# Compressed attention by head pairs, masks as products, and respread pieces of stick-breaking and delta rule

## The chip, the cores and the metric

The kernel runs on one core of one Trainium2 chip. What counts is the device time of one execution in microseconds (us). The core has five engines that run their own instruction streams and meet through semaphores: TensorE (PE in the profile), VectorE (DVE), ScalarE (ACT), GpSimd (POOL) and SyncE (SP, here only DMA issue). A product on PE has two halves, the load of the stationary operand (PEld) and the pass of the moving one (PE).

## What is computed

Two transformer blocks follow each other, each of two layers, on 512 tokens of width 1024. The first block mixes latent attention, sparse attention (DSA, 4 heads) and retention, then a feed-forward part. The second block mixes a gated delta rule (6 heads), a native sparse attention (NSA, 6 heads on 2 key groups) and stick-breaking attention (4 heads), then a convolutional feed-forward part. The parts that the change touches, from the reference:

```python
# NSA: compressed keys and values, one per 16 tokens (31 of them), then two causal attentions
kc = compress(rope(kv(k_cmp), positions), pe_k, ck_w1, ck_w2)
vc = compress(kv(v_cmp), pe_v, cv_w1, cv_w2)
s_c = jnp.einsum('bqgrd,bigd->bgrqi', qb, kc).astype(f32) * scale
p_c = masked_softmax(s_c, cmp_end[None, :] <= tq[:, None])
o_c = jnp.einsum('bgrqi,bigd->bqgrd', p_c.astype(vc.dtype), vc)
# stick-breaking, per head
log_stick = lax.cumsum(log_1m, axis=3, reverse=True) - log_1m
a = jnp.where(strict, jnp.exp(jax.nn.log_sigmoid(z) + log_stick), 0.0)
return jnp.einsum('bhqk,bkhd->bqhd', a.astype(v.dtype), v)
# gated delta rule, per chunk of 64 tokens: S is the state
S_t = exp(g_t) (I - beta_t k_t k_t^T) S_{t-1} + beta_t k_t v_t^T
```

## The kernel before

The program is a row of stages. Each stage is a block in which every engine has its own instruction list, and a barrier closes it, so a stage ends with its slowest engine. The order inside a stage is written out by hand: the loops below are it. Token tiles are 128 rows (four tiles, `TT`), a PSUM bank holds 512 columns. In each layer of the second block the stages around the change follow in this order.

**Compressed attention** (`turned_and_compressed`). PE turns queries and keys, makes the compressed keys and values and then, for each of 6 heads and 4 token tiles, the scores against 31 compressed keys (L3256, contraction over 64 rows, 31 moving columns). DVE adds the mask (L3368), takes maxima, subtracts (L3373), ACT exponentiates (L3320), DVE masks again (L3378) and signals `masked`. Then the tail: for each head PE turns four tiles of weights (L3269), ACT copies them out of PSUM (L3325), PE multiplies them with the values (L3278), DVE scales the result into its place (L3390). Beside it ACT and DVE split the queries into a high and a low part (L3295, L3348) for the next stage. PE is kept moving before the tail by 26 transposes without use (L164).

**NSA attention** (`softmax_attention`, name `nsa`). 12 heads (6 heads, two key sets), four tiles each, software pipelined over units of one head and tile: scores as two reduced-precision products (L2362), for tiles 2 and 3 the causal mask as a third product (L2365), for tiles 0 and 1 the mask as a DVE addition in PSUM (L2400), maximum (L2401, DVE), exponential (L2431, ACT), transposes (L2374, PE), copy (L2440, ACT), output products (L2384, PE). The first block's DSA stage is the same function with four heads, where tiles 1 and 2 have product masks and tiles 0 and 3 additions.

**Stick-breaking** (`stick_breaking`). 16 units of head and key tile. PE: scores (L3422), running sums (L3433, L3441), and, five units after the last unit of a head, its ten output products in one piece (L3453). DVE: mask (L3495), softplus (L3504), total (L3512), and beside it the NSA head norm in large pieces (L3514, L3517, four L3521, L3526). The running sums wait for the softplus.

**Delta rule** (`gated_delta`). First `transpose_tiles` turns 12 sets of 128 columns (L486) while DVE scales keys and queries (L3874, L3875), POOL makes two faded copies of the keys (L3878, L3880), and the turned sets are copied out of PSUM by ACT (even sets, L508) and DVE (odd sets, L525). Then `delta_inverse`, where POOL starts with a memset (L2983) and one addition per head (L2988), and `delta_scan`, which alone reads the faded keys.

## Time and profile before

| | us |
|---|---|
| three runs, median (lowest to highest) | 3344.66 (3342.47 to 3351.53) |
| the profiled execution, its own time | 3343.76 |
| its span, first to last instruction | 3341.8 |
| PE busy in the span | 3172.3 (95%) |
| DVE busy | 1839.2 (55%) |
| ACT busy | 1303.3 (39%) |
| POOL busy | 390.2 (12%) |
| mean granted TensorE clock | 0.978 of full |

A busy time is the time in which an engine had an instruction in work. PE is busy nearly always, but its time is not fixed: at half of the clock the same product takes twice as long and is still busy. So the profile is read stage by stage, with the granted clock beside the busy time, and with what each engine waited for. Stages are found by the names of their tensors: `cmp` for the compressed attention, `nsa`, `stick`, `b_work` and `b_kbe` for the delta rule.

### The profile page before, as it was taken

The numbers are of one execution on the slowest core, as the hardware profiler recorded it, in microseconds if no ns is written. First come the engines' busy times: TensorE is split into PE (matmuls) and PEld (weight loads), VectorE is DVE, ScalarE is ACT, GpSimd is POOL, SyncE is SP. The second block draws the span as 40 slices with busy tenths as digits, with TensorE's granted clock in tenths as the row PEclk, the third lists the DMA queues.
The fourth block names the chain that finished last, engine by engine and source line by source line (L and its number), as shares of the span: only waits on it lengthen the run. The fifth ranks groups of instructions, "written<-read, shape, count | busy, mean of one in ns | idle before, by whom it ended". The sixth has DMA issues, their size and how long they took to land. (4 is left out here: it accounts for less than half of the span.)

```text
span 3341.8 us, 48972 instructions
## 1 busy us (share of the span) xinstructions
PE 3172.3 (95%) x19264; PEld 2667.0 (80%) x19264; DVE 1839.2 (55%) x3260; ACT 1303.3 (39%) x2690; POOL 390.2 (12%) x354
## 2 busy tenths in 40 slices
PE   8999999999999999979999999999899989999996
PEld 6877788877877888868877888888788868888885
DVE  4875443436864434247466457474475565474644
ACT  4454433334354424234363333233443643332324
POOL 1021000000030000003013302010003034010100
PEclk9999999999999999989899999999999899999998
DMA  4111222222202222132100123222232000232231
GB/s 167 54 51 39 89 96 94 88 78 82 71 1 76 101 88 101 38 123 96 51 1 2 40 76 98 96 101 86 73 104 76 1 1 15 82 103 93 92 103 39
DMA packets 37341, 239.54 MB, mean 72 GB/s; under 512 B 4464, under 2 KB 5232, under 8 KB 15088
## 3 DMA queue, kind: packets, MB, share of 16 engines
q1 hardware_dynamic: 36528, 234.21, 20.6%
q8 instruction: 158, 2.59, 0.3%
q10 hardware_dynamic: 576, 2.10, 0.2%
q14 instruction: 79, 0.65, 0.1%
HBM read 234.19 MB, written 2.10 MB: 71 GB/s over the span
## 5 line engine op out<-in xcount | busy, mean ns | idle before, releaser
L265 PE MATMUL ps<-b_hl,bff_whl 128*128 128x512 f32 x704 | 274.2, 389 | 3.1 <-DVE b_hl L665 3.1
L267 PE MATMUL ps<-b_hl,bff_whl 128*128 128x512 f32 x704 | 274.0, 389 | 0.0
L266 PE MATMUL ps<-b_hl,bff_whl 128*128 128x512 f32 x704 | 273.9, 389 | 0.0
L248 DVE SCALAR_TENSOR_TENSOR bff_whl<-ring,b_cols,bff_whl 128x512 fp32r<-128x512 f32 (+1 forms) x224 | 153.2, 745 | 197.3 <-ACT bff_whl L235 197.0
L245 DVE TENSOR_TENSOR aff_whl<-ring,aff_whl 128x512 fp32r<-128x512 f32 x160 | 99.9, 687 | 224.8 <-ACT aff_whl L233 224.8
L235 ACT ACTIVATE bff_whl<-ring,b_cols 128x512 fp32r<-128x512 f32 (+1 forms) x224 | 136.6, 681 | 176.4 <-PE ps L267 176.4
L266 PE MATMUL ps<-aff_whl,a_u 128*128 128x512 f32 x512 | 204.3, 399 | 0.0
L265 PE MATMUL ps<-a_hl,aff_whl 128*128 128x512 f32 x512 | 200.8, 392 | 3.1 <-DVE a_hl L665 3.1
L265 PE MATMUL ps<-aff_whl,a_u 128*128 128x512 f32 x512 | 201.8, 394 | 0.0
L267 PE MATMUL ps<-aff_whl,a_u 128*128 128x512 f32 x512 | 200.7, 392 | 0.0
L266 PE MATMUL ps<-a_hl,aff_whl 128*128 128x512 f32 x512 | 200.5, 392 | 0.0
L267 PE MATMUL ps<-a_hl,aff_whl 128*128 128x512 f32 x512 | 200.5, 392 | 0.0
L265 PE MATMUL ps<-ain_whl,a_hl 128*128 128x512 f32 (+3 forms) x512 | 189.3, 370 | 8.4 <-issue 5.2
L233 ACT CAST aff_whl<-ring 128x512 fp32r<-128x512 f32 x160 | 87.5, 620 | 278.6 <-PE ps L267 272.5
L266 PE MATMUL ps<-ain_whl,a_hl 128*128 128x512 f32 (+3 forms) x512 | 186.3, 364 | 0.0
L267 PE MATMUL ps<-ain_whl,a_hl 128*128 128x512 f32 (+3 forms) x512 | 186.0, 363 | 0.0
L245 DVE TENSOR_TENSOR bff_whl<-ring,bff_whl 128x512 fp32r<-128x512 f32 x128 | 84.7, 722 | 144.3 <-ACT bff_whl L233 144.2
L265 PEld LDWEIGHTS ps<-b_hl,bff_whl 128*128 128x128 f32 x704 | 132.2, 188 | 31.0 <-DVE b_hl L665 3.6
L248 DVE SCALAR_TENSOR_TENSOR aff_whl<-ring,a_gains,aff_whl 128x512 fp32r<-128x512 f32 x128 | 87.6, 747 | 125.5 <-ACT aff_whl L235 125.3
L267 PEld LDWEIGHTS ps<-b_hl,bff_whl 128*128 128x128 f32 x704 | 132.2, 188 | 27.4
L266 PEld LDWEIGHTS ps<-b_hl,bff_whl 128*128 128x128 f32 x704 | 132.2, 188 | 27.3
L233 ACT CAST bff_whl<-ring 128x512 fp32r<-128x512 f32 x128 | 70.4, 621 | 210.4 <-PE ps L267 202.9
(521 smaller groups left out, 7804.7 us busy)
## 6 DMA issues: line engine op xcount, KB each, us to landing
ring<-in_a_w_ff SPq DMA_DIRECT2D x64, 1024.0 KB, 4.8
ring<-in_b_w_up SPq DMA_DIRECT2D x32, 1024.0 KB, 5.0
ring<-in_a_w_in SPq DMA_DIRECT2D x16, 1024.0 KB, 5.4
ring<-in_b_w_down SPq DMA_DIRECT2D x16, 1024.0 KB, 4.8
ring<-in_b_w_in_att SPq DMA_DIRECT2D x12, 1024.0 KB, 4.9
ring<-in_b_w_up SPq DMA_DIRECT2D x16, 768.0 KB, 4.2
ring<-in_b_w_in_conv SPq DMA_DIRECT2D x12, 768.0 KB, 4.4
ring<-in_a_w_out SPq DMA_DIRECT2D x8, 1024.0 KB, 4.9
```

The source lines that it names most:

```text
L233: self.c.nc.scalar.copy(self.part(j, 0, k), src[:, k, :]).then_inc(self.hi_made, 1)
L235: self.c.nc.scalar.activation(self.part(j, 0, k), src[:, k, :], ACT.Copy, scale=g[:, row + k:row + k + 1]).then_inc(self.hi_made, 1)
L245: self.c.nc.vector.tensor_tensor(self.part(j, 1, k), src[:, k, :], self.part(j, 0, k).bitcast(F32), ALU.subtract).then_inc(self.lo_made, 1)
L248: self.c.nc.vector.scalar_tensor_tensor(out=self.part(j, 1, k), in0=src[:, k, :], scalar=g[:, row + k:row + k + 1], in1=self.part(j, 0, k) ...
L265: nc.tensor.matmul(bank, sh, mh, start=start, stop=False)
L266: nc.tensor.matmul(bank, sh, ml, start=False, stop=False)
L267: return nc.tensor.matmul(bank, sl, mh, start=False, stop=stop)
```

## The change

It changes only the stages named above. No load, no weight product and no feed-forward part is touched.

1. Compressed attention by pairs of heads. Keys and values of two heads stand on the diagonal of one block (`kc` 128 rows by 2 times 32 columns, `vc` 64 rows by 128 columns), the rest is zero. Scores are 12 products over 128 rows and 64 columns in place of 24 over 64 rows and 31 columns; the tail has three turns instead of six. POOL clears the blocks, DVE fills them with four small copies each. The query lows of heads 2 to 5 move into the NSA stage.
2. All causal and selection masks of the NSA and DSA stages are products; DVE's additions there are gone.
3. Stick-breaking: the output products of a head are issued in three pieces over three units, its copy out of PSUM one unit later, and the norm's large DVE pieces are cut by token tile.
4. Delta rule: DVE copies out only sets 2, 5 and 8 of the twelve, ACT the others; the faded keys are made by POOL in eight pieces inside `delta_inverse`, the second from the product of beta and decay (`beg`).

```diff
@@ turned_and_compressed, PE
-                for h in range(H):
-                    b, gr = HD * (h % 2), h // NSA_R
-                    bank, at = score_at(h)
+                for a in range(A):
+                    bank, at = score_at(a)
                     for t in range(TT):
-                        ins = nc.tensor.matmul(c.ps[:, bank, at + t * N:at + (t + 1) * N],
-                                               qT[b:b + HD, h // 2, t * P:(t + 1) * P],
-                                               kcT[b:b + HD, gr * N:(gr + 1) * N], start=True, stop=True)
+                        ins = nc.tensor.matmul(c.ps[:, bank, at + t * 2 * NW:at + (t + 1) * 2 * NW],
+                                               qT[:, a, t * P:(t + 1) * P],
+                                               kc[:, a].rearrange("p b n -> p (b n)"), start=True, stop=True)
...
@@ DVE, the diagonal blocks and the two query lows that stay
+                for b in range(2):
+                    r, ones = slice(HD * b, HD * (b + 1)), group_of(b).index(1)
+                    ins = spread([(kc[r, 0:ones, b, 0:N], 0), (kc[r, ones:A, b, 0:N], 1)],
+                                 c.ps[r, SMALL, 128:128 + G * N].rearrange("p (g n) -> p g n", g=G))
...
+                query_low(0)
+                query_low(1)
                 for i in range(13, len(turns), 2):
                     keep(i)
...
@@ attentions, the NSA heads
-                              lambda j, a=v + h // NSA_R * HD: proj[:, j, a:a + HD], lambda t: c.causal if t < 2 else None,
+                              lambda j, a=v + h // NSA_R * HD: proj[:, j, a:a + HD], lambda t: None,
...
-                              lambda t: (mask_product[0][:], mask_product[1][:]) if t >= 2 else None)
+                              lambda t: (mask_product[0][:], mask_product[1][:]))
+                beside=lambda dve, done, i: queries.low(dve, done, 2 + i // 4) if i in (0, 4, 8, 12) else None,
+                ready=lambda pe, done, h: pe.wait_ge(done, h - 1) if 2 <= h < NSA_H else None)
@@ stick_breaking, PE
-                    u = i - 5
-                    if 0 <= u < U and units[u][1] == 0:
+                    for late, tiles in ((5, (0, 1)), (6, (2,)), (7, (3,))):
+                        u = i - late
+                        if not (0 <= u < U and units[u][1] == 0):
+                            continue
@@ stick_breaking, DVE
-                    if i == 3:
-                        nc.vector.tensor_tensor(sq[:], xo, xo, ALU.mult).then_inc(squared, 1)
+                    if 2 <= i < 2 + TT:
+                        t = i - 2
+                        nc.vector.tensor_tensor(sq[:, t], xo[:, t], xo[:, t], ALU.mult).then_inc(squared, 1)
...
@@ gated_delta
-            nc.gpsimd.tensor_tensor(as4(g["kel"]), k4, wide(g["el"]), ALU.mult)
-            pool.wait_ge(made, 1)
-            nc.gpsimd.tensor_tensor(as4(g["kbe"]), as4(g["kb"]), wide(g["eg"]), ALU.mult)
-        transpose_tiles(c, "deltaT", jobs, faded, None, scaled, wait_scaled)
+            nc.gpsimd.tensor_tensor(g["beg"], g["beta"], g["eg"], ALU.mult)
+        transpose_tiles(c, "deltaT", jobs, faded, None, scaled, wait_scaled, (2, 5, 8))
```

The order of the instructions shows it at three places. The first is PE from the compressed scores to the start of the NSA stage. `cmpkcT` and `cmpkc` are the compressed keys, `cmps` the weights, `cmppT` the turned weights, `cmpvcmp` and `cmpvc` the values. Before:

```order
L3256 MATMUL ps<-cmpkcT,b_qT 128x31 x24
L3215 MATMUL ps<-const_b,b_proj 128x128 x12
L164 MATMUL ps<-const_b 128x128 x26
L3269 MATMUL ps<-const_b,cmps 31x128 x8
L3278 MATMUL ps<-cmpvcmp,cmppT 128x64 x4
L3269 MATMUL ps<-const_b,cmps 31x128 x4
L3278 MATMUL ps<-cmpvcmp,cmppT 128x64 x4
```

(Three more such pairs follow, and a last product group of eight.) In the changed kernel:

```order
L3262 MATMUL ps<-cmpkc,b_qT 128x64 x12
L3221 MATMUL ps<-const_b,b_proj 128x128 x12
L164 MATMUL ps<-const_b 128x128 x26
L3275 MATMUL ps<-const_b,cmps 64x128 x8
L3285 MATMUL ps<-cmpvc,cmppT 128x128 x4
L3275 MATMUL ps<-const_b,cmps 64x128 x4
L3285 MATMUL ps<-cmpvc,cmppT 128x128 x8
```

The tail is now 12 transposes and 12 products of twice the moving columns, in place of 24 and 24.

The second place is DVE in the first units of the stick-breaking stage, where `sticksq` and `stickssq` belong to the NSA norm. Before:

```order
L3512 TENSOR_TENSOR ps<-ps,stickz 128x256
L3514 TENSOR_TENSOR sticksq<-b_mix 128x1536
L3495 TENSOR_TENSOR stickz<-ps,stickhide 128x128
L3504 SCALAR_TENSOR_TENSOR sticksp<-stickz,sticke 128x512
L3512 TENSOR_TENSOR ps<-ps,stickz 128x384
```

In the changed kernel, the same stretch:

```order
L3545 TENSOR_TENSOR ps<-ps,stickz 128x256
L3548 TENSOR_TENSOR sticksq<-b_mix 128x384
L3528 TENSOR_TENSOR stickz<-ps,stickhide 128x128
L3537 SCALAR_TENSOR_TENSOR sticksp<-stickz,sticke 128x512
L3545 TENSOR_TENSOR ps<-ps,stickz 128x384
L3548 TENSOR_TENSOR sticksq<-b_mix 128x384
L3552 TENSOR_REDUCE stickssq<-sticksq 128x6
```

A quarter of the squares stands where the whole stood, and the other quarters are in the units around.

The third is POOL from the turning stage of the delta rule into `delta_inverse`. Before:

```order
L3878 TENSOR_TENSOR b_kel<-b_qkv,b_g_el 128x1536
L3880 TENSOR_TENSOR b_kbe<-b_work,b_g_eg 128x1536
L151 UNCONDITIONAL_BRANCH
L2981 UNCONDITIONAL_BRANCH
L2983 MEMSET b_work 64x24x64
L2988 TENSOR_TENSOR b_work<-b_work,const_b 128x256 x6
```

In the changed kernel:

```order
L3921 TENSOR_TENSOR b_beg<-b_g_beta,b_g_eg 128x24
L151 UNCONDITIONAL_BRANCH
L2982 UNCONDITIONAL_BRANCH
L2984 MEMSET b_work 64x24x64
L3926 TENSOR_TENSOR b_kel<-b_qkv,b_g_el 128x384 x4
L2991 TENSOR_TENSOR b_work<-b_work,const_b 128x256
L3926 TENSOR_TENSOR b_kbe<-b_qkv,b_beg 128x384
L2991 TENSOR_TENSOR b_work<-b_work,const_b 128x256
```

The two large products have left the turning stage and stand in eight quarters behind its closing barrier (the two branches), the last four between the additions of the heads.

## Rows read from the trace of the kernel before

**Rows 1.** The page: busy time and share; granted TensorE clock in 40 slices.

```profile
PE 3172.3 (95%) x19264; PEld 2667.0 (80%) x19264; DVE 1839.2 (55%) x3260; ACT 1303.3 (39%) x2690; POOL 390.2 (12%) x354
...
PEclk9999999999999999989899999999999899999998
```

**Rows 2.** Busy time by stretch, stick-breaking of both layers: engines, then PEclk, DMA.

```profile
1729.00:1781.00 52.00, 46.90 (x195) 30.21 (x194) 31.17 (x63) 29.07 (x65) 13.93 (x18) 0.87 0.00 1
...
2669.00:2717.00 48.00, 42.34 (x194) 27.34 (x194) 30.92 (x62) 29.08 (x65) 13.93 (x18) 0.96 0.00 1
```

**Rows 3.** The same view in stretches of 2 us, compressed tail, both layers.

```profile
1650.00:1652.00 2.00, 2.00 (x15) 1.69 (x14) 1.11 (x2) 0.57 (x1) 0.00 (x0) 0.86 0.00 0
...
2588.00:2590.00 2.00, 2.00 (x10) 1.43 (x9) 0.91 (x2) 0.00 (x0) 0.00 (x0) 0.50 0.00 0
```

**Rows 4.** Timeline, compressed stage, second layer: start, us, engine, line, [idle before].

```profile
2575.20 3.41 PE L3256 MATMUL ps<-cmpkcT,b_qT 64*128 64x31 f32 x48 [0.61 <-DVE cmpkcT L3359]
...
2584.01 0.93 DVE L3378 TENSOR_TENSOR cmps<-cmps,const_b 128x744 f32<-128x744 f32 x1 [1.84 <-ACT cmps L3320]
...
2587.05 1.96 PE L3278 MATMUL ps<-cmpvcmp,cmppT 31*128 31x64 f32 x8 [1.00 <-ACT cmppT L3325]
...
2588.95 1.06 PE L3269 MATMUL ps<-const_b,cmps 128*31 128x128 f32 x4
...
2602.31 0.42 DVE L3390 TENSOR_TENSOR b_mix<-ps,cmpst 128x256 f32<-128x256 f32 x1 [0.56 <-PE ps L3278]
...
2603.05 0.44 PE L2362 MATMUL ps<-b_khi,b_qhl 128*128 128x128 f32 x1 [0.78 <-PEq L151]
```

**Rows 5.** Timeline, the same tail in the first layer.

```profile
1646.13 0.93 DVE L3378 TENSOR_TENSOR cmps<-cmps,const_b 128x744 f32<-128x744 f32 x1 [3.13 <-ACT cmps L3320]
...
1649.18 1.10 PE L3278 MATMUL ps<-cmpvcmp,cmppT 31*128 31x64 f32 x8 [1.00 <-ACT cmppT L3325]
...
1663.30 0.44 PE L2362 MATMUL ps<-b_khi,b_qhl 128*128 128x128 f32 x1 [0.78 <-PEq L151]
```

**Rows 6.** Timeline, products of the new shapes' kind at full clock.

```profile
2567.74 3.91 PE L3226 MATMUL ps<-b_kv2T,ring 128*128 128x66 f32 x32
...
2728.21 1.16 PE L2846 MATMUL ps<-b_work 64*128 64x128 f32 x8
...
2729.20 1.05 PE L2846 MATMUL ps<-b_dqT,b_work 64*128 64x128 f32 x8
```

**Rows 7.** Timeline, one head of the NSA stage in its steady state.

```profile
2628.11 0.30 DVE L2400 TENSOR_TENSOR ps<-ps,const_b 128x128 f32<-128x128 f32 x1 [1.14 <-PE ps L2362]
...
2629.95 0.22 PE L2365 MATMUL ps<-b_causalr,b_identr 128*128 128x128 f32 x1
...
2630.01 0.28 PE L2374 MATMUL ps<-const_b,nsap 128*128 128x128 f32 x1
...
2631.83 0.41 PE L2374 MATMUL ps<-const_b,nsap 128*128 128x128 f32 x2 [0.35 <-ACT nsapT L2440]
```

**Rows 8.** Stick-breaking: PE's waits (total, times, longest) of both layers; one DVE piece.

```profile
PE ps L3433 <- DVE sticksp L3504: 3.9, 5, 1.2
...
PE ps L3433 <- DVE sticksp L3504: 4.7, 7, 1.2
...
2675.45 1.75 DVE L3514 TENSOR_TENSOR sticksq<-b_mix 128x1536 f32<-128x1536 f32 x1
```

**Rows 9.** Timeline, turning stage of the delta rule, second layer.

```profile
2717.19 2.76 POOL L3878 TENSOR_TENSOR b_kel<-b_qkv,b_g_el 128x1536 f32<-128x1536 f32 x1 [9.19 <-POOLq L151]
2717.21 4.36 DVE L3874 TENSOR_TENSOR b_work<-b_qkv,b_g_beta 128x1536 f32<-128x1536 f32 x1 [0.72 <-PEq L151]
...
2721.49 1.75 DVE L3875 TENSOR_TENSOR b_work<-b_qkv,b_g_eg 128x1536 f32<-128x1536 f32 x1
...
2725.55 1.28 DVE L525 TENSOR_SCALAR b_qeT<-ps 128x512 f32<-128x512 f32 x2
...
2727.15 1.13 PE L2839 MATMUL ps<-const_b,b_g_gcum 128*128 128x128 f32 x8 [0.85 <-PEq L151]
```

210 lines of the change are left out of this document (121 added, 89 removed).

## The prediction

> **What bounds the kernel now.** The page comes first. PE is busy for 3172.3 of 3341.8 us and DVE for 1839.2 [rows 1], so over the whole program a faster DVE, ACT or POOL is worth nothing by itself. The row of granted clocks reads 9 nearly everywhere, with a few 8s [rows 1]. Since a product at half of the clock is busy for twice the time, the next view is the one by stretches, for the stages of the change. There PE's clock is 0.96 in the stick-breaking of layer 2 and 0.87 in that of layer 1, and the second takes 52 us in place of 48 with the same work [rows 2]. In the compressed tail PE is busy without a gap and its clock is 0.50, the lower level (1.2 of 2.4 GHz), in layer 2, and on its way there in layer 1 [rows 3]. So three things can be won: PE work and its time at half clock (compressed tail), waits of PE (stick-breaking, NSA), and a stage that another engine ends (the turning stage of the delta rule, where DVE's last copies end [rows 9]). Every term below occurs in each of two layers. The sums are made against the profiled execution, 3343.76 us; the median of the runs is 0.9 us above it, which is less than I can resolve.
>
> **1. The compressed tail.** The path is: DVE masks the weights (end of L3378), ACT copies turned weights, PE multiplies and turns, DVE scales the last result (L3390), the barrier, first NSA product. In layer 2 the mask ends at 2584.01 + 0.93 = 2584.94 and NSA starts at 2603.05, 18.1 us later [rows 4]. In layer 1 it is 1647.06 to 1663.30, 16.2 us [rows 5]. The first eight value products take 1.96 us in layer 2 and 1.10 in layer 1 [rows 4, 5]: the clock had already fallen in the one, and in the other it fell within 1650 to 1652, where 0.86 as a mean puts the fall 0.56 us before the end, at 1651.4 or 4.4 us after the mask [rows 3].
>
> The new tail starts like the old: eight turns, and the first product 2.1 us after the mask (2587.05 and 1649.18 [rows 4, 5]), because ACT's copy of the turned weights stands before it. Then come four products, four turns and eight products, the products now 64 rows by 128 columns. That form is in the trace: the next group of L2846 starts 0.99 us after one of eight records, which are four products, since a full-precision product has two records (24 scores are 48) [rows 4, 6]. The old group of 64 columns costs 1.10, so the price goes by the product and not by its columns, and at half clock it is 1.96 [rows 4, 5]: I take 1.0 us for four new products and 2.0 at half clock. Four turns are 1.06 us at half clock [rows 4] and 0.53 at full. So PE needs 1.0 + 0.53 + 2.0 = 3.5 us at full clock and 7.1 at half. To that the 2.1 us before it, 0.1 to reach DVE, about 0.7 for a last scaling of 512 columns (an estimate from 0.42 for 256 [rows 4] and 0.64 for a plain copy of 512 [rows 9]) and 0.3 from its end to the next stage, as 2602.73 to 2603.05 now [rows 4]. The tail is 6.8 us at full and 10.3 at half clock. The mask itself comes 0.3 us later, for four small copies more on DVE (about 0.1 each); the scores pay part of that back: 24 products of 64 rows cost 3.41 us (48 records [rows 4]), 12 over 128 rows are 24 records of at most 0.122 (3.91/32 [rows 6]), 2.9 us.
>
> Layer 2, with the clock falling when it did: 18.1 - 10.3 - 0.3 = 7.5 saved (11.0 at full clock). Layer 1, with the fall 4.4 us after the mask, which leaves only the last group at half: end at 7.9, 16.2 - 7.9 - 0.3 = 8.0 (5.6 all at half, 9.1 at full). I take **-15.5**, between -13 and -20. A full clock at the start of NSA would add up to 4. The query lows that stay on DVE hide under ACT's exponentials; if that cover were gone, they would cost 0.64 each [rows 9], 2.6 in all.
>
> On the scores one rule bears. The row shows 3.41/48 = 0.07 us a record for contractions over 64 rows and 0.122 for 128 [rows 4, 6]. The Trainium skill, page "TensorEngine Tiling (Array Packing)", section "Key Properties", says that different tiles of the array can load and multiply in parallel. By it the block diagonal, which fills the whole array with half zeros, gives away an overlap that the old form had. The trace agrees in that a 64-row record is cheaper, but not at more than the halved count gives back. By the rule alone this step would be a wash, by the rows a gain of 0.5 us a layer; no more than 1 us of the sum hangs on it.
>
> **2. Stick-breaking.** PE waits for the softplus five times for 3.9 us in layer 1 and seven times for 4.7 in layer 2, the longest 1.2 [rows 8]. What delays the softplus is that DVE works off pieces of up to 1.75 us for the norm (L3514 [rows 8]) ahead of it; now the pieces are a quarter, 0.44. The rest of the waits lies at the first units after a head, where running sums are due quickly while the ten output products stand in one piece at another place; they are now spread over three units, which gives the chain to softplus more cover. I take two thirds of the waits, 3.0 + 2.6 = 5.6. Then the clock: 0.87 over 52 us is 13.5 us at half, 0.96 over 48 is 3.8 us [rows 2], and each costs half of itself, 8.7 together. Its fall follows stretches in which PE stands, so fewer waits mean fewer falls; I take 4, which is what layer 1 is longer than layer 2 [rows 2]. Together **-9.5**. Bounds: -2, if the wait moves to the ACT link of the chain, since ACT (29 us of 48) is as loaded as DVE (31 [rows 2]); -15, if all 8.6 of waits and 6 of the clock return.
>
> **3. The turning stage of the delta rule.** DVE's product L3874 takes 4.36 us while POOL's L3878 (2.76) starts with it, and L3875, the same size, takes 1.75 afterwards [rows 9]: 2.76 + 1.6. Without POOL's product there both take 1.75, DVE is free 2.6 us earlier, and copies out three sets in place of six (0.64 each [rows 9], 1.9 less). DVE would then be done 4.5 us earlier, at about 2722.4; but ACT now copies nine sets and PE's turns are not faster, so these are late next. With nine at 0.6 or so in a row behind the first turned sets I put the end at about 2724 instead of 2726.83 (2725.55 + 1.28). That is 2.9 a layer, **-5.8**, between -4 and -6.5. The eight quarters on POOL (2.76/4 = 0.69 each) stand behind the memset in the inverse stage, which POOL enters idle (9.19 us of idle time before L3878 [rows 9] shows how little it has to do around here). If they hit DVE's products there, eight per layer and half of them on the path, it would be 4 × 0.7 × 2 = 5.6 us back; I hold this out of the sum and put it into the range.
>
> The lock shows here as 4.36 against 1.75 [rows 9]. The Trainium skill, page "SBUF — State Buffer", section "🔬 SBUF: two separate sides", states that a DVE instruction with two SBUF inputs and a GpSimd instruction that reads SBUF hold a shared pair of ports exclusively, for the whole instruction. The trace agrees. By it moving POOL's products is worth something only where DVE has no such product beside them; by its strict reading the quarters would give back up to 5.6 us.
>
> **4. NSA.** 24 heads (12 in each layer). Tiles 0 and 1 get a mask product each, as tiles 2 and 3 have: 0.06 us by the distance to the next product (2629.95 to 2630.01), at most 0.12 [rows 6, 7]. DVE loses two additions of 0.30 per head, the one at 2628.11 behind its own wait, and PE's wait of 0.35 for ACT's copy once per head [rows 7] is the end of the chain that ran through them. A head then gives 0.35 - 0.24 = 0.11 to 0.35 - 0.12 = 0.23; over the 20 heads without a late query low 2.2 to 4.6, say 2.6. Four heads (two in each layer) do a query low (0.64 [rows 9]) together with the norm work of the stage before, some +0.4 each, +1.6. **-1**, from -5 to +8 (no wait returned, all products at 0.12, and 0.64 lost in each of four heads).
>
> **5. DSA of the first block.** The same with 4 heads in each of 2 layers, 8 × 0.1: **-0.8**, from -3 to +1.
>
> The sum is 15.5 + 9.5 + 5.8 + 1 + 0.8 = 32.6, and 3343.76 - 32.6 = **3311**.
>
> **The rivals.** *Waits only move.* In stick-breaking the softplus waits for ACT, not DVE, and the clock stays low through the whole short tails. Then -12 (tail), -2 (stick), -4 (delta), 0 (NSA, DSA): 18 us, 3326. For it: ACT and DVE are nearly equally busy there [rows 2], and the clock in the tail was 0.50 [rows 3]. Against it: the largest wait has the length of a DVE piece [rows 8].
>
> *The clock holds.* With denser products and fewer stands PE keeps 2.4 GHz in tail, NSA start and stick-breaking: 20 + 4 + 15 + 6.5 + 2 = 47 us, 3297. For it: the clock fell late in layer 1's tail [rows 3]. Against it: the wait before the tail (1.00 us [rows 4, 5]) remains.
>
> *The mask products are no bargain.* NSA and DSA lose 9, and the others stand at their lower ends, 13 + 2 + 4: 10 us, 3334, within 0.3%. For it: PE is the bound, and this gives it work. Against it: 0.06 us in the row [rows 7].
>
> *Slower.* The place is the NSA stage behind the shorter tail, the mechanism the clock: the tail leaves it at 0.50 [rows 3], and if it stays there, each us of a bound PE loses half. To be slower by 10 us it must lose 33 + 10 = 43, so the clock would have to stay low for over 86 us in all. Against it: the slices of the page after both tails read 9 [rows 1], behind the same 0.50.
>
> **How the numbers follow.** Forecast 3311: 0.51 (its own range 3303 to 3320). Waits only move, 3326: 0.25. The clock holds, 3297: 0.17. Mask products no bargain, 3334: 0.05. Slower: 0.02. The range for 8 in 10 goes from 3296 to 3328: it takes in the second and third case and the 5.6 us of the lock. 0.3% (10 us) is about what a measurement of this kernel can tell from no change; faster by more has 0.51 + 0.25 + 0.17 = 0.93, within it 0.05, slower 0.02.
>
> **What the profile after would show.** Step 1: 7 to 10 us from the mask to the first NSA product, where 18.1 and 16.2 stand. Step 2: PE's waits for the softplus at some 1.5 us a layer in place of 3.9 and 4.7, and the clock of the layer 1 stretch near 0.97. If they are shorter but new waits for ACT stand beside them, the first rival is right. Step 3: L3874's successor at 1.75 us and a last copy 3 us earlier; a POOL quarter beside a lengthened DVE product in the inverse stage would show the lock. Step 4: the 0.35 us before L2374 gone, no new wait before it, and mask slots of 0.06. The forecast is wrong above all if the value products of 128 columns are not 0.25 us each, or if the clock in tail and stick-breaking behaves otherwise than it did.

## The result, and the profile after

The changed kernel takes 3300.15 us in the median of three runs (3296.66 to 3302.26), where the kernel before took 3344.66. The ratio is 0.9869, with a 95% interval of 0.9845 to 0.9892. That is faster, as forecast, and inside the range of 3296 to 3328, but the gain is 44.5 us where 33.7 were forecast. The profiled execution has a span of 3298.4 us in place of 3341.8, that is 43.4 less.

The page first: the row of PE's busy time, and the granted clock in 40 slices, to be read against [rows 1].

```profile
PE 3144.2 (95%) x19216; PEld 2651.6 (80%) x19216; DVE 1812.1 (55%) x3220; ACT 1302.5 (39%) x2692; POOL 391.2 (12%) x374
...
PEclk9999999999999999989999999999999999999998
```

PE has 28.1 us less of busy time with only 48 records fewer, so most of that is not work that went away but work that ran at a higher clock; the other 15.3 us are time in which PE stood, that is, had nothing in work. The stages tell where. This is the view by stretches with one stretch per stage, in the order DSA, compressed attention, NSA, stick-breaking, turning stage of the delta rule, each in its second layer. The columns after the comma are the busy times of PE, PEld, DVE, ACT and POOL with their records, then the clock, the DMA share and GB/s. The kernel before:

```profile
988.09:1013.98 25.89, 22.06 (x169) 19.72 (x169) 15.91 (x35) 14.70 (x49) 7.72 (x4) 1.00 0.00 1
2557.07:2603.05 45.98, 41.50 (x374) 37.53 (x375) 24.91 (x44) 18.03 (x31) 3.56 (x2) 0.82 0.14 47
2603.05:2669.59 66.54, 61.88 (x488) 58.02 (x489) 42.24 (x120) 44.12 (x145) 0.00 (x0) 0.97 0.00 1
2669.59:2717.21 47.62, 42.34 (x195) 27.34 (x195) 30.64 (x62) 29.05 (x65) 13.95 (x19) 0.96 0.00 1
2717.21:2727.15 9.94, 6.74 (x57) 6.06 (x57) 9.62 (x8) 3.59 (x6) 7.00 (x3) 1.00 0.00 0
```

The changed kernel:

```profile
983.48:1007.49 24.01, 23.04 (x176) 20.79 (x177) 13.26 (x27) 14.62 (x49) 7.72 (x4) 1.00 0.00 1
2531.82:2569.39 37.57, 32.74 (x318) 30.11 (x319) 21.41 (x46) 16.34 (x28) 5.04 (x5) 0.88 0.17 57
2569.39:2634.26 64.87, 62.69 (x512) 60.67 (x513) 38.71 (x100) 43.67 (x145) 0.00 (x0) 0.97 0.01 1
2634.26:2677.33 43.07, 40.28 (x194) 26.52 (x195) 30.62 (x70) 29.17 (x65) 13.28 (x19) 1.00 0.00 1
2677.33:2683.94 6.61, 6.31 (x57) 6.10 (x57) 5.30 (x5) 4.84 (x9) 0.27 (x2) 1.00 0.00 0
```

With the first layers, read from the same view:

| stage | before, layer 1 / 2 | after, layer 1 / 2 | forecast, both | measured, both |
|---|---|---|---|---|
| compressed attention | 46.14 / 45.98 | 37.56 / 37.57 | -15.5 | -17.0 |
| stick-breaking | 51.57 / 47.62 | 43.06 / 43.07 | -9.5 | -13.1 |
| turning stage of the delta rule | 9.94 / 9.94 | 6.61 / 6.61 | -5.8 | -6.7 |
| NSA | 66.58 / 66.54 | 65.10 / 64.87 | -1 | -3.2 |
| DSA | 27.38 / 25.89 | 24.09 / 24.01 | -0.8 | -5.2 |
| sum | | | -32.6 | -45.0 |
| all other stages | | | 0 | +1.6 |

Every term has the forecast sign and every one is larger than forecast. A stage's length times what its mean clock lacks of 1 is what the lower clock cost there; over these stages that is about 32 us before and 13 after, so some 19 of the 45.0 us are clock. That part is the one that varies between executions of the same stage, and each number here is from one execution. The other stages differ by up to 3 us in either direction, mostly with their clock (the stretch between the two layers took 661.3 us before and 664.3 after). One small stage ahead of the DSA search takes 6.83 us in place of 6.63 at full clock in every kernel with the change, a cost of 0.4 us in all that I had not seen.

The compressed tail, on PE and then DVE, second layer:

```profile
2559.63 1.42 PE L3275 MATMUL ps<-const_b,cmps 128*64 128x128 f32 x8 [2.23 <-DVE cmps L3407]
2561.56 2.07 PE L3285 MATMUL ps<-cmpvc,cmppT 64*128 64x128 f32 x8 [0.51 <-ACT cmppT L3332]
...
2564.56 3.78 PE L3285 MATMUL ps<-cmpvc,cmppT 64*128 64x128 f32 x16
2569.39 0.45 PE L2363 MATMUL ps<-b_khi,b_qhl 128*128 128x128 f32 x1 [1.05 <-PEq L151]
...
2558.51 1.07 DVE L3407 TENSOR_TENSOR cmps<-cmps,const_b 128x248 f32<-128x248 f32 x3 [0.20 <-ACT cmps L3327]
```

The mask ends at 2559.58 and NSA starts at 2569.39: 9.8 us, where [rows 4] gave 18.1. A group of four products of 128 columns takes 2.07 us at half clock, where I had taken 2.0. Ahead of the tail PE stands for 2.23 us, in both layers. In the kernel before it stood there too, for 2.09 us in the second layer, and for only 0.85 in the first, which no row of mine had shown:

```profile
1647.12 1.06 PE L3269 MATMUL ps<-const_b,cmps 128*31 128x128 f32 x8 [0.85 <-DVE cmps L3378]
...
2585.00 1.06 PE L3269 MATMUL ps<-const_b,cmps 128*31 128x128 f32 x8 [2.09 <-DVE cmps L3378]
```

### The profile page after: what moved, and what is told of

The parts are those of the page before. It is cut to its first block and busy times, and to the rows that moved or that the text cites. A ratio compares the mean times of both kernels' runs of the same rounds, so it can differ in the third digit from the quotient of the medians.

```text
span 3298.4 us, 48870 instructions
## 1 busy us (share of the span) xinstructions
PE 3144.2 (95%) x19216; PEld 2651.6 (80%) x19216; DVE 1812.1 (55%) x3220; ACT 1302.5 (39%) x2692; POOL 391.2 (12%) x374
```

## Stick-breaking: which of the two pieces, and what the clock adds

Two kernels undo one part of the change each. The first gives DVE its large pieces back:

```diff
-                    if 2 <= i < 2 + TT:
-                        t = i - 2
-                        nc.vector.tensor_tensor(sq[:, t], xo[:, t], xo[:, t], ALU.mult).then_inc(squared, 1)
+                    if i == 3:
+                        nc.vector.tensor_tensor(sq[:], xo, xo, ALU.mult).then_inc(squared, 1)
...
+                    if i == 12:
+                        nc.vector.tensor_tensor(xo, xo, ssq[:].unsqueeze(3).broadcast_to(shape), ALU.mult)
```

> The changed kernel with one part undone: in stick-breaking DVE does the norm of the stage before in its large pieces again (one of 1536 columns for the squares, one for their sums, four for the gain, one of 1536 for the last factor). The output products of a head stay spread over three units. Reference points for the stage, from barrier to barrier: 51.6 and 47.6 us before (granted clock 0.87 and 0.96), 43.1 and 43.1 after (clock 1.00 in both). Theory D (the large DVE pieces delay the softplus, PE stands, and the clock falls after it): the two waits of about 1.2 us return, the clock falls again in at least one layer, the stage takes 46 to 50 us, and the kernel is 5 to 12 us slower than the changed one. Theory P (the ten output products in one piece are what starves the chain to the softplus): the stage stays at 43 to 44.5 us at clock 1.00, and the kernel within 3 us of the changed one.

It is slower than the changed kernel: 0.9924 of the kernel before (0.9902 to 0.9945), where the changed one has 0.9869, some 13 us by the medians and more than the 5 to 12 expected. The two layers run the same instructions, and this is what the view by stretches has for them, and for three stretches within the second:

```profile
1713.27:1757.83 44.56, 40.28 (x195) 26.52 (x195) 30.57 (x62) 29.11 (x65) 13.95 (x19) 1.00 0.00 1
2630.98:2684.80 53.82, 49.62 (x194) 31.97 (x195) 31.11 (x61) 29.26 (x65) 13.94 (x19) 0.81 0.00 1
2643.00:2646.00 3.00, 1.98 (x8) 1.01 (x7) 2.69 (x5) 1.45 (x3) 0.71 (x2) 1.00 0.00 0
2646.00:2649.00 3.00, 2.38 (x6) 1.52 (x6) 2.25 (x5) 2.87 (x9) 2.06 (x3) 0.54 0.00 0
```

And the piece of PE's timeline ahead of the fall, with the two large DVE pieces behind which the softplus stood:

```profile
2639.86 1.10 PE L3462 MATMUL ps<-sticksp,const_b 128*128 128x512 f32 x2 [1.19 <-DVE sticksp L3537]
2644.93 0.67 PE L3462 MATMUL ps<-sticksp,const_b 128*128 128x256 f32 x2 [1.02 <-DVE sticksp L3537]
2646.86 1.62 PE L3462 MATMUL ps<-sticksp,const_b 128*128 128x384 f32 x2 [0.62 <-DVE sticksp L3537]
...
2636.83 1.75 DVE L3547 TENSOR_TENSOR sticksq<-b_mix 128x1536 f32<-128x1536 f32 x1
2642.25 1.74 DVE L3550 TENSOR_REDUCE stickssq<-sticksq 128x24 f32<-128x1536 f32 x1
```

PE's waits for the softplus are 3.9 us in six places in either layer, in place of 2.4 us in the changed kernel. In layer 1 that costs 44.56 - 43.06 = 1.5 us and nothing else. In layer 2 the same waits were followed by a granted clock of 0.50 (the lower level, 1.2 GHz) from 2646 to about 2667, and the stage took 10.8 us longer than in the changed kernel, 9.3 of them by the clock. So a wait has a small price that is certain and a large one that comes in some executions of a stage and not in others.

The second kernel has the small DVE pieces and the ten output products in one piece again:

```diff
-                    for late, tiles in ((5, (0, 1)), (6, (2,)), (7, (3,))):
+                    for late, tiles in ((5, (0, 1, 2, 3)),):
...
-                    if 0 <= i - 4 < U and units[i - 4][1] == 1 and units[i - 4][0] >= 1:
+                    if 0 <= i - 3 < U and units[i - 3][1] == 1 and units[i - 3][0] >= 1:
```

> The counterpart: the changed kernel with the ten output products of a head in one piece again, five units after its last unit, and their copy out of PSUM one unit earlier; DVE's norm pieces stay cut by token tile. Theory D: the stage stays at 43 to 44.5 us, clock 1.00. Theory P: the stage goes back to 46 to 50 us, the waits of PE for the softplus rise from 2.4 us a layer to 3.5 or more, and the clock falls below 0.97 in at least one layer. If both parts are needed, this one and its counterpart each give about half, 45 to 46 us.

```profile
1712.87:1757.80 44.93, 40.72 (x195) 26.17 (x195) 30.44 (x70) 28.93 (x65) 13.27 (x19) 1.00 0.00 1
2631.52:2676.44 44.92, 40.71 (x194) 26.17 (x195) 30.43 (x70) 28.92 (x65) 13.27 (x19) 1.00 0.00 1
```

The stage takes 1.9 us more in both layers, with PE's waits at 3.6 us in eight places and one more of 0.3, and the clock stays full. The total does not show it (0.9869, interval 0.9847 to 0.989): 3.7 us is less than such a comparison can tell. Both parts are worth something, and neither theory has it alone. At full clock the stage of the kernel before takes 45.9 us: that is measured, in the run with 34 transposes below, whose stick-breaking is that of the kernel before and whose second layer had clock 1.00. So of the 13.1 us, 2 x 2.9 = 5.8 come back at full clock, nearly all of them waits, and 7.3 are clock.

The 7.3 belongs to this pair of executions. In the run with 34 transposes the same stage took 47.60 and 45.94 us, and against these the changed kernel gains 7.4 us, of which 1.7 are clock. What holds over all runs is how often the clock fell: in three of the four layers with the old stage, and in one of the twenty layers of the ten kernels that have the new one (44.71 us at clock 0.96, in the second layer of the next experiment).

## DSA: one addition of 512 columns

Here the forecast was farthest off. The experiment gives tile 3 its addition on DVE back, and only that (a third edit, not shown, lets the search write this tile's mask where the addition reads it):

```diff
-                                        lambda t: None,
+                                        lambda t: search.tile(3) if t == 3 else None,
...
-                                        mask_products=lambda t: (identr[:], search.mask(t) if t else causalr[:]))
+                                        mask_products=lambda t: (identr[:], search.mask(t) if t else causalr[:]) if t < 3 else None)
```

> The changed kernel with the search mask of tile 3 in the DSA stage added by DVE again (512 columns in PSUM) while tile 0 keeps its mask product. The DSA stage took 27.4 and 25.9 us before, 24.1 and 24.0 after, where I had forecast a gain of only 0.4 us a layer. Theory A (the one addition of 512 columns, 0.70 us, once per head in front of the maximum, made PE wait for ACT four to five times): PE's waits for ACT go back to 2.5 us or more and the stage to 25.5 us or more. Theory B (tile 0's addition of 0.30 was as much to blame, since it stands at the head's change): waits of 1.0 to 1.5 us, stage near 25 us.

```profile
276.48:303.64 27.16, 23.93 (x173) 21.48 (x173) 15.60 (x31) 14.66 (x49) 7.72 (x4) 0.94 0.00 1
989.36:1016.08 26.72, 23.51 (x173) 21.05 (x173) 15.51 (x31) 14.73 (x49) 7.72 (x4) 0.95 0.00 1
```

The stages take 27.16 and 26.72 us where the changed kernel has 24.09 and 24.01, and PE waits for ACT's copy four times for 2.4 us, longest 1.1, and once for its exponential for 0.4. The kernel is at 0.9891 of the one before (0.9867 to 0.9916), which by itself can't be told from the changed kernel; the stage can. The cause is to be seen in the trace of the kernel before, DVE and PE:

```profile
1007.30 0.70 DVE L2400 TENSOR_TENSOR ps<-ps,a_score 128x512 f32<-128x512 f32 x1 [0.69 <-PE ps L2362]
...
1009.94 0.63 PE L2374 MATMUL ps<-const_a,dsap 128*128 128x128 f32 x4 [1.11 <-ACT dsapT L2440]
```

The addition stands in front of the maximum, the maximum in front of the exponential, and so on to PE; at the end of the stage nothing is left to run beside that chain, and its whole length is PE's wait. A clock of 0.95 over 26.7 us is a tenth of it at half clock, 1.3 us lost, so at full clock the stage would be near 25.4 (worked out, not measured). Then 1.4 of the 1.9 us between 25.89 and 24.01 are tile 3's, and the rest tile 0's. Theory A held. The clock fell in both layers of this run and in one of the kernel before.

## The turning stage: the lock and the split

Two kernels again, one with POOL's copies back in the stage, one with the old division of the copies out of PSUM:

```diff
         def faded(pool, made):
-            nc.gpsimd.tensor_tensor(g["beg"], g["beta"], g["eg"], ALU.mult)
+            nc.gpsimd.tensor_tensor(as4(g["kel"]), k4, wide(g["el"]), ALU.mult)
+            pool.wait_ge(made, 1)
+            nc.gpsimd.tensor_tensor(as4(g["kbe"]), as4(g["kb"]), wide(g["eg"]), ALU.mult)
```

> The changed kernel with POOL's two faded copies of the keys back in the turning stage of the delta rule, each in one instruction, and no quarter in the inverse stage. The split of the copies out of PSUM stays the new one (DVE sets 2, 5 and 8). Turning stage 9.94 us before, 6.61 after. Theory lock (POOL's product holds DVE's off): DVE's first product takes about 4.4 us again in place of 1.75, and the stage takes 9 us or more, because POOL itself (2.8 + 2.8 us and a wait) also ends late; the kernel is 4 to 6 us slower. Theory split (what mattered was DVE copying out three sets in place of six): the stage takes 7 to 7.5 us. The same run takes the eight quarters out of the inverse stage (77.5 and 74.6 us after, 76.0 and 76.3 before): if they cost anything there, it falls by up to 2.8 us a layer; I expect under 0.5 at the same clock.

```diff
-        transpose_tiles(c, "deltaT", jobs, faded, None, scaled, wait_scaled, (2, 5, 8))
+        transpose_tiles(c, "deltaT", jobs, faded, None, scaled, wait_scaled)
```

> The changed kernel with the old division of the copies out of PSUM in the turning stage of the delta rule (DVE the odd sets, six of twelve), POOL's products staying in the inverse stage. Turning stage 6.61 us after, 9.94 before. By my forecast DVE is free 2.6 us earlier than before without POOL's product, so the old split alone gives about 7.3 us (9.94 - 2.6); the new split would then be worth 0.7 us a layer. Theory lock alone: 7.0 to 7.6. Theory split: 9 us or more.

DVE's first product of the stage in the changed kernel, and then DVE's and POOL's with POOL's copies back:

```profile
2677.33 1.83 DVE L3915 TENSOR_TENSOR b_work<-b_qkv,b_g_beta 128x1536 f32<-128x1536 f32 x1 [0.71 <-PEq L151]
```

```profile
2672.99 4.37 DVE L3915 TENSOR_TENSOR b_work<-b_qkv,b_g_beta 128x1536 f32<-128x1536 f32 x1 [0.72 <-PEq L151]
...
2672.98 2.77 POOL L3921 TENSOR_TENSOR b_kel<-b_qkv,b_g_el 128x1536 f32<-128x1536 f32 x1 [8.69 <-POOLq L151]
2677.44 4.21 POOL L3923 TENSOR_TENSOR b_kbe<-b_work,b_g_eg 128x1536 f32<-128x1536 f32 x1 [1.69 <-DVE b_work L3915]
```

The stage takes 8.99 us in both layers with POOL's copies, 7.42 with the old split alone, 6.61 in the changed kernel. From 9.94 the lock is worth 2.5 us a layer and the new split 0.8; counted in the other order, by the run with POOL's copies, it is 2.4 and 0.9. The lock works both ways: POOL's second copy started beside DVE's and took 4.21 us in place of 2.8, and then ended the stage. The totals of both runs (0.9879 and 0.988, each about 0.986 to 0.990) do not differ from the changed kernel's; 4.8 and 1.6 us can't be told by them, and the verdicts rest on the stage.

The quarters cost nothing that can be seen in the inverse stage. With them it took 77.5 and 74.6 us, without them 75.7 and 74.3, and the long one had clock 0.98. At full clock it is 74.6 with and 74.3 and 75.7 without; I had 5.6 us in the range for a collision there, which did not come. One thing stays open. The scan behind it took 28.4 us at full clock in all six layers of the three kernels without quarters. In the kernels with them it did so in twelve of 22 layers, and in ten the clock fell at its start or just ahead of it and it took 29.9 to 30.1, as in the second layer of the changed kernel. PE's waits in the scan are the same in both, and no run tells whether the quarters have a part in it.

## The compressed tail: what the transposes without use are worth

The stand of 2.23 us ahead of the tail raised the question whether it brings the clock down. Three runs change the number of transposes without use, 26 in both kernels:

```diff
-                c.stay_busy(pe, SMALL, 26)
+                c.stay_busy(pe, SMALL, 45)
```

> The changed kernel with 45 in place of 26 transposes without use ahead of the compressed tail. In the changed kernel PE stands for 2.23 us between the last of them and the first turn of the weights, and the granted clock falls to 0.50 within about 1.8 us of the tail's start in layer 1 and 0.6 in layer 2. One of them takes 0.115 us, so 19 more fill the gap. Theory gap (the clock falls because PE stood just before): the clock stays full through the tail, which goes from 9.8 us (mask to first NSA product) to about 7, the first NSA units run at full clock too, and the kernel gets 6 to 10 us faster. Rival (the clock falls for what the tail itself is: small products with short stands for ACT's copy): no change within 2 us, the clock still 0.50 in the tail.

> The changed kernel with none of the 26 transposes ahead of the tail: PE stands for about 5.2 us there. Theory gap: the clock falls at once or earlier than now and stays at 0.50 at least as long into the NSA stage, which costs up to 3 us a layer. Rival (these transposes have no effect, the clock falls for another reason): tail and NSA start as now, within 1 us.

> The kernel before with 34 in place of 26 transposes without use ahead of the compressed tail; PE stood there for 0.85 us, and the granted clock fell to 0.50 some 2 us into the tail in layer 2 and 4.4 us in layer 1. Theory gap (the stand ahead of the tail brings the clock down): the tail of six turns runs at full clock, about 11 us from the mask to NSA in place of 18.1 and 16.2, and the kernel is 8 to 14 us faster than the one before, so that half of what the pairs of heads brought could be had without them. Rival (the short stands inside the tail, 1.0 us for ACT's copy, bring it down too): the clock falls a few us into the tail all the same, and less than 4 us are gained.

With 45 the compressed stage takes 34.48 us in both layers in place of 37.57, and the kernel is at 0.9856 (0.9837 to 0.9874); its median of 3290.84 us is below the changed kernel's 3300.15, but the intervals overlap. Against the kernel with none of them, which was run at the same time, its runs lie apart (3288.03 to 3292.62 against 3298.20 to 3301.54). By stages it gains 7.1 us. The tail of its second layer on PE, and the granted clock around it (start and end of the stretch, its length, PE's busy time, the clock):

```profile
2550.67 1.06 PE L3275 MATMUL ps<-const_b,cmps 128*64 128x128 f32 x8 [0.16 <-DVE cmps L3407]
2552.60 1.16 PE L3285 MATMUL ps<-cmpvc,cmppT 64*128 64x128 f32 x8 [0.86 <-ACT cmppT L3332]
2554.24 2.05 PE L3285 MATMUL ps<-cmpvc,cmppT 64*128 64x128 f32 x16
2557.34 0.30 PE L2363 MATMUL ps<-b_khi,b_qhl 128*128 128x128 f32 x1 [1.05 <-PEq L151]
```

```profile
2557.30:2559.30 2.00, 1.90 (x11) 0.88 0.00 0
2559.30:2561.30 2.00, 2.00 (x10) 0.50 0.00 0
2561.30:2563.30 2.00, 2.00 (x17) 0.77 0.00 0
```

The tail runs at full clock, 6.7 us from mask to NSA. But the clock still falls, only later: 1.5 us into NSA, after the stands of 0.86 and 1.05. So the gap theory holds for the tail, and its second half (the first NSA units run at full clock too) does not: NSA gains 0.5 and 0.4 us.

With none of them the stage takes 37.55 and 37.56, to a hundredth what it takes with 26, though PE stands for 5.07 us:

```profile
2557.47 1.92 PE L3274 MATMUL ps<-const_b,cmps 128*64 128x128 f32 x8 [5.07 <-DVE cmps L3406]
```

The clock then falls within the stand, 2.7 and 1.9 us before the mask ends. With 26 it falls 1.6 and 0.6 us after it, and the tail is at half clock either way. As they stand in the changed kernel the 26 are worth nothing.

In the kernel before, eight more brought the stand ahead of the tail from 0.85 to 0.27 us in the first layer and from 2.09 to 0.11 in the second (the expectation took 0.85 for both). They did not help: the ratio is 0.9999 (0.9983 to 1.0016), and the tail takes 16.8 and 16.5 us in place of 16.2 and 18.1. PE in the tail of its second layer:

```profile
2588.05 1.10 PE L3278 MATMUL ps<-cmpvcmp,cmppT 31*128 31x64 f32 x8 [1.00 <-ACT cmppT L3325]
...
2589.64 1.64 PE L3278 MATMUL ps<-cmpvcmp,cmppT 31*128 31x64 f32 x8
2591.20 1.06 PE L3269 MATMUL ps<-const_b,cmps 128*31 128x128 f32 x4
```

The first group of products runs at full clock (1.10 us), the second is caught by the fall (1.64), and the rest of a tail of 16 us is at half clock. The rival was right there. All the runs together say how far the stand matters. In the sixteen layers with a stand of 2.09 us or more the clock had fallen at the latest 2.4 us after the mask. In the eleven with 0.85 or less it fell 3.8 to 8.8 us after it, or, in one, not at all. One layer of the changed kernel with POOL's copies lies between: there the clock fell for a while in the scores, PE's work took longer, the stand shrank to 1.45 us, and the tail ran at full clock (6.7 us). A tail of 6.7 us can be over before such a late fall and one of 16 us can't, but the fall at 3.8 to 4.4 would have caught the short one as well. What decides between 4 and 8 us stays open. The Trainium skill, page "TensorE: Matmul & The Clock Gate", section "🔬 Part 1: The HAM clock gate (the "warmup" mystery)", says that a clock gate sets PE's rate by how busy it has been recently. The runs agree in direction: each fall shown here follows stands. They also show that equal stands do not always bring one, as the two layers of the first experiment did.

## The query lows

> The changed kernel with the low parts of queries 2 to 5 made in the compressed tail (two before the first scaling of results, two before the second) and not beside the first NSA units. NSA stage now 65.1 and 64.9 us, mask to NSA 9.8. My forecast put the cost of the late query lows in NSA at 0.8 us a layer. If that holds, NSA falls by 0.8 to 64.2 and the tail, where DVE waits 2 us before each scaling, grows by under 0.5. Rival (they are free in NSA, since PE is at low clock in its first units): NSA unchanged within 0.3 us.

```diff
                 for a in range(A):
+                    if a == 0:
+                        query_low(2)
+                        query_low(3)
+                    if a == 1:
+                        query_low(4)
+                        query_low(5)
                     dve.wait_ge(outs, a + 1)
```

```profile
1651.23:1715.04 63.81, 62.59 (x513) 61.07 (x513) 36.09 (x97) 43.57 (x145) 0.00 (x0) 0.96 0.01 1
2566.15:2629.88 63.73, 62.52 (x513) 61.01 (x513) 36.09 (x97) 43.56 (x145) 0.00 (x0) 0.96 0.01 1
```

NSA falls by 1.3 and 1.1 us to 63.8 and 63.7. The compressed stage stays at 37.57 in layer 2; in layer 1 it took 39.21, with clock 0.85 in place of 0.89. There the clock fell once more, during the scores (0.68 over 1632 to 1634 and 0.50 over 1634 to 1636), which is ahead of the mask and so ahead of the lows: they had no part in it, and the tail itself took 9.8 us as before. So the late query lows cost 1.2 us a layer (I had 0.8), and the 24 mask products with DVE's additions gone give 66.5 - 63.8 = 2.8 a layer.

## A faster kernel

The last three runs put the findings together. The first, 45 transposes and all lows in the compressed stage, fits the two runs before it:

> The changed kernel with 45 transposes ahead of the tail and all query lows made in the compressed stage (two before the first scaling of results, one before each of the others). From the runs with one of the two: the compressed stage 34.5 us, NSA 64.5 - 1.2 = 63.3 us, so 2 x (3.1 + 0.4 + 1.2) = 9.4 us less than the changed kernel by stages; if the lows no longer hide under the shorter tail, up to 1.4 us a layer come back.

```diff
-                c.stay_busy(pe, SMALL, 26)
+                c.stay_busy(pe, SMALL, 45)
...
                 for a in range(A):
+                    if a == 0:
+                        query_low(2)
+                        query_low(3)
+                    else:
+                        query_low(3 + a)
```

It takes 3287.27 us, 0.9837 (0.9815 to 0.9859). The compressed stage is at 35.50 and 35.23, so 0.7 to 1.0 of the lows' 1.2 came back: under the shorter tail DVE no longer has the room. (In the first layer the clock also fell within the tail, 4.4 us after the mask.)

The second goes for what then ends last, ACT's chain: the load of the exponential table after its casts, and four casts between the exponentials and the copy of the turned weights.

> The compressed stage with the link of the chain that now ends last shortened. In the changed kernel ACT's load of the exponential table (1.28 us) starts only when its two query casts are through and stands before the exponentials, and four casts of 2.52 us stand between the exponentials and the copy of the turned weights. Here the table that also holds the logarithm is asked for ahead of ACT's idle time of 4.8 us, all six casts stand in that idle time, ACT keeps the last turned set in place of DVE, DVE's masks follow the exponentials at once, POOL makes the lows of queries 2 to 5 after the mask, and 36 transposes without use stand ahead of the tail. Theory: the mask comes 1.3 us earlier, mask to NSA takes about 6 us in place of 9.8 (7 with more transposes alone), so the compressed stage takes 32 to 33 us in place of 37.6; NSA 63.3; the load of the table at the start of stick-breaking is gone (hidden or up to 1.3 us). Together 12 to 16 us less than the changed kernel by stages. Rivals: POOL's four lows (about 1 us each) end after PE and hold the stage open, 34 us or more; or ACT's casts, started earlier, hold up PE's last turned sets.

```diff
                 silu(1)
+                nc.scalar.preload_act_table_set("natural_log_exp_and_others")
...
+                for f in range(H):
+                    query_high(f)
+                for i in range(12, len(turns)):
+                    keep(i)
...
+                pool.wait_ge(masked, 1)
+                for f in range(2, H):
+                    queries.low(pool, q_los, f, nc.gpsimd)
```

It takes 3288.64 us, 0.9842 (0.982 to 0.9864), no better, with 35.55 and 34.91 us for the stage. That is the rival's number (34 or more) but not its mechanism: POOL was done at 2559.04, before PE's last product at 2560.18, and held the stage up by way of DVE. DVE and POOL after the mask, second layer:

```profile
2555.35 0.97 DVE L3413 TENSOR_TENSOR cmpst<-cmpst,b_proj 128x24 f32<-128x24 f32 x1
2556.35 0.23 DVE L3416 CAST b_identr<-const_b 128x128 fp32r<-128x128 f32 x1
2556.49 1.29 DVE L3416 CAST b_causalr<-const_b 128x128 fp32r<-128x128 f32 x1
2557.71 0.68 DVE L3421 TENSOR_TENSOR b_mix<-ps,cmpst 128x512 f32<-128x512 f32 x1
2558.42 1.17 DVE L446 TENSOR_TENSOR b_qhl<-b_qT,b_qhl 64x512 fp32r<-64x512 f32 x1
...
2553.68 5.36 POOL L446 TENSOR_TENSOR b_qhl<-b_qT,b_qhl 64x512 fp32r<-64x512 f32 x4 [22.08 <-DVE cmps L3407]
```

In the changed kernel the first of them takes 0.18 us and the second cast 0.22. POOL's four pieces take 1.26 to 1.35 us each, and each of the two ends less than 0.1 us after a piece that had begun before it. The first cast began together with a piece and took its usual 0.23. The scaling that reads PSUM (L3421, 0.68) is not touched. The third value products waited 0.85 us for the first scaling. Moreover, the table load stood ahead of ACT's casts of the keys, and PE's scores waited 1.82 us in place of 1.03.

The third mends both: no lows on POOL, the load behind the key casts, all casts and lows of the queries in idle time early in the stage.

> A mend of the run before. There POOL's four lows (1.34 us each, not 1) stretched DVE's small instructions beside them (a cast from 0.22 to 1.29 us) and held the third scaling up, and the table load, put ahead of ACT's key casts, let PE wait 0.8 us longer for the compressed keys. Here POOL does nothing, the table load stands behind the key casts, and all six casts and six lows stand in idle time of ACT and DVE that the trace of the changed kernel shows early in the stage (3.0 us of ACT twice, 5.4 and 2.3 us of DVE); 36 transposes without use ahead of the tail, all turned sets from the thirteenth on kept by ACT, as there. Theory: the mask comes 1.3 us earlier than in the changed kernel, mask to NSA takes 6.1 us or less, the compressed stage 32 to 33 us (37.6 in the changed kernel, 34.5 with more transposes alone), NSA 63 to 63.7, the stick-breaking stage 43.1 as before or less by its table load. By stages 12 to 14 us less than the changed kernel, some 3 to 5 less than the run with 45 transposes and lows in the tail. Rival: the extra casts delay ACT's first activation or a key copy on which PE waits, and the hidden products move back by as much; then the stage stays at 34 us or more.

```diff
                 for i in (0, 2, 4, 6):
                     keep(i)
+                for i in (4, 5, 6):
+                    wait_kept(act, i)
+                for f in range(4):
+                    query_high(f)
                 silu(0)
                 keep(7)
                 keep(8)
+                for f in range(4, H):
+                    query_high(f)
                 silu(1)
                 keep(9)
                 keep(10)
+                nc.scalar.preload_act_table_set("natural_log_exp_and_others")
```

```profile
1610.22:1642.73 32.51, 30.20 (x328) 28.45 (x329) 23.56 (x49) 16.84 (x29) 5.03 (x5) 1.00 0.19 66
2522.60:2555.11 32.51, 30.20 (x328) 28.45 (x329) 23.55 (x49) 16.84 (x29) 5.03 (x5) 1.00 0.19 66
2555.11:2617.42 62.31, 60.62 (x513) 58.79 (x513) 35.99 (x97) 43.58 (x145) 0.00 (x0) 1.00 0.01 1
```

It takes 3283.34 us (3281.02 to 3286.36), 0.9824 of the kernel before (0.9805 to 0.9843). Its runs lie wholly below the 3296.66 to 3302.26 of the changed kernel, though those were made at another time; its interval does not meet the changed kernel's, but it does meet that of the first of these three. The compressed stage is 32.51 us in both layers (37.6 in the changed kernel, 46 before), with 6.1 us from mask to NSA (2549.01 to 2555.11), as expected. NSA took 63.14 us in layer 1 and 62.31 in layer 2, where the clock did not fall at all. The table load at the start of stick-breaking is gone too, and that stage still takes 43.08 us: the load had been hidden.

## Why the prediction was right, and where its sizes were off

The sign of every part held, and the order of the three large ones; in the DSA the path that gave the gain had not been read. The sum was 12 us short, at five terms, and the time came to lie inside the range with that shortfall.

- **Compressed tail**, forecast 15.5, measured 17.0 for the stage. The second layer's tail came out as worked out: 10.3 us forecast at half clock, 9.8 measured. In the first layer the step "with the fall 4.4 us after the mask" was wrong: the clock fell 1.6 us after the mask (it is 0.90 as a mean over 1637 to 1639, and the mask ends at 1636.96), and that tail took 9.8 too, not 7.9. The 4.4 had been read from a tail ahead of which PE stood for only 0.85 us, and it stood so briefly because the clock had fallen already during that layer's scores, so that PE's work lasted longer. The old second layer, with a stand of 2.09 us and a fall 1.7 us after the mask, was the pattern for both. What made up for the error is the same fall in the scores: with it the old first layer took 29.9 us from the stage's start to the mask, and now it is 27.8. Part of this may be luck, because such a fall in the scores of the first layer also occurs in three of the later kernels with the new scores.
- **Stick-breaking**, forecast 9.5, measured 13.1. The term for waits had the right size (5.6 forecast, 5.8 measured), but it was not made up as forecast: at full clock PE's waits for the softplus fell from 4.6 to 2.4 us a layer, by half and not by two thirds, and a wait of 0.3 for ACT and 0.4 of busy time did the rest. The forecast put "the largest wait" at "the length of a DVE piece", but set 1.2 beside 1.75 us; the run with the large pieces shows waits of 1.19 and 1.02 behind pieces of 1.75 and 1.74. The term for the clock was too small for this pair of executions: of the 8.7 us that it cost I took 4 back, and 7.3 came. That they were 7.3 is chance, since by the other execution of the old stage it is 1.7. That fewer waits mean fewer falls is borne out, by three in four against one in twenty layers. The undoing of one part showed what half clock follows there, stands within some us of each other.
- **Turning stage**, forecast 5.8, measured 6.7. The lock was worth what the row said (2.6 forecast, 2.5 measured). ACT's nine copies ended last, as forecast, but at 2681.93 + 1.58, 6.2 us after the stage's start, where I had put 6.8: priced at 0.6 us one by one, they take 1.09 in pairs.
- **NSA**, forecast 1, measured 3.2. Two terms were mis-sized against each other: the masks gave 2.8 us a layer, not 1.3, since a mask product added only about (62.5 - 61.9)/24 = 0.03 us to PE's busy time (at mean clocks of 0.96 and 0.97) and PE's waits for ACT fell from 3.7 us in 11 places to 0.4; the late lows cost 1.2 us a layer, not 0.8.
- **DSA**, forecast 0.8, measured 5.2: the one real miss. "The same with 4 heads, 8 x 0.1" carried the price of an addition of 128 columns over to a stage in which one of them has 512 (0.70 us, not 0.30) and which ends behind it. PE's waits for ACT there were 3.4 us a layer in the trace of before, and I had not read them. At full clock the stage gave some 1.9 us a layer (25.89 to 24.01 in the second); the other 1.5 us are a fall of the clock in the old first layer.

No run undoes the pairs of heads or NSA's masks by themselves: their parts are read from the stages, before and after, while stick-breaking, DSA and the turning stage have runs of their own.

Of the rivals, "waits only move" fell: where waits went, no new ones for ACT appeared. "The clock holds" came true in stick-breaking and DSA, not in the tail, which fits a result between the forecast and it. The two small cases fell as well; the mask products cost less than their lower bound. The price of the value products held, and the rule on tiles of the array had no visible consequence: the new scores took 2.86 us for 24 records, 0.12 each as in [rows 6], where [rows 4] had 3.41 for 48, a gain of 0.55 us a layer. Whether the old record was cheaper for its 64 rows or for its 31 columns, no run separates.

## What to carry to other kernels

A wait of the engine that bounds the kernel has two prices, its length and the clock that may fall behind it; take the first as certain and the second as a chance, and read the clock by stage before and after. Price an operation that moves off a chain by its own size in each stage that shares the code, above all at the stage's end, where nothing covers the chain. A clock that fell once may have fallen by chance: take how often from several executions, and how long from one. Look at what an engine waits for in front of a meeting point: here the transposes that were to keep PE moving ended 2.2 us too early (and 2.1 already in one layer of the old kernel). Filling that gap, shortening the other engine's chain and moving the query lows out of NSA were together worth as much again as a third of the change.

## What the runs showed of the hardware

The same instructions with the same waits (3.9 us in six places) kept full clock in one layer and fell to half in the other, 44.56 and 53.82 us. In each of the sixteen layers in which PE stood for 2.09 us or more ahead of the compressed tail, the clock had fallen at the latest 2.4 us after the tail's start, with 26 transposes without use in front of the stand (fourteen layers) and with none (two). With the stand filled the tail can be over first, and the fall then comes in the next stage, 1.5 us into NSA in the run with 45 transposes.

A small instruction of DVE between SBUF tensors that began during one of POOL's (1.26 to 1.35 us) ended with it: 0.97 us for 24 columns (0.18 alone), 1.29 for a cast of 128 (0.22 alone). One that reads PSUM took its usual 0.68, and a cast that began together with POOL's piece its usual 0.23. I had known that of large products with two SBUF inputs [rows 9]. The Trainium skill, page "SBUF — State Buffer", section "🔬 SBUF: two separate sides", names the casts' kind as well, an operation of DVE in its two-port mode, which an fp32 copy within SBUF sets off; the trace agrees, for the one cast that began after POOL.
